# Three moves in a single-core transformer kernel: forget weights scaled later, gate logits after the third chunk, a bank sum ahead of the first convolution

## The reference, cut to what matters

```python
# first block, gated linear attention: the input projection and the gate
proj = x @ w_in
q, k, v, g, a1 = jnp.split(proj, [...], axis=-1)
log_a = jax.nn.log_sigmoid((a1 @ w_a2 + b_a).astype(jnp.float32)) / GATE_TAU
...
b = jnp.cumsum(to_chunks(log_a), axis=3)
q_dec = qc * jnp.exp(b); k_dec = kc * jnp.exp(-b); k_end = kc * jnp.exp(b_last - b)

# second block, each of 2 layers: norm, projection with the forget columns in it
u = rms_norm(h, attn_norm_w[i])
proj = u @ w_in[i]                      # f_logit: 8 of its columns

# second block, each of 2 layers: the feed-forward network
up = u @ w_up
a, g = up[..., :D_FF_2], up[..., D_FF_2:]
a = causal_depthwise_conv(a, conv_w, conv_b)
return (jax.nn.gelu(a, approximate=False) * g) @ w_down
```

## Time and profile before

| | us |
|---|---|
| median of 3 runs | 1370.71 (1370.24 to 1370.98) |
| the profiled run | 1370.33 |
| its span (first to last instruction) | 1368.6 |
| outside the span | 1.7 |

### The profile page before, as it was taken

How to read it: one execution, slowest core, us unless ns; L and a number is a source line. 1 busy time by engine, 2 the same in 40 slices (tenths; PEclk the granted TensorE clock), 3 DMA queues, 4 the chain that set the end, 5 groups by cost and what they waited for, 6 DMA issues and landing times.

```text
span 1368.6 us, 21813 instructions
## 1 busy us (share of the span) xinstructions
PE 1321.9 (97%) x8766; PEld 1187.6 (87%) x8766; DVE 915.9 (67%) x1091; ACT 667.0 (49%) x764; POOL 31.2 (2%) x52
## 2 busy tenths in 40 slices
PE   7899999998999999998999999999999999999997
PEld 6898888887986888887998989999989988999997
DVE  3746755566455765667666687777696768877775
ACT  6345544445455544445445554444655455544454
POOL 0000000000011000000200000000020000000000
PEclk9999999999999999999999999999999999999999
DMA  9534655554533455553533355555545324555520
GB/s 374 203 124 154 228 196 195 191 195 138 183 121 109 181 203 185 184 184 118 198 131 117 126 182 184 184 184 184 175 143 187 137 84 164 198 184 184 184 93 32
DMA packets 33490, 229.85 MB, mean 168 GB/s; under 512 B 3728, under 2 KB 3984, under 8 KB 6032
## 3 DMA queue, kind: packets, MB, share of 16 engines
q1 hardware_dynamic: 31536, 220.21, 45.9%
q10 hardware_dynamic: 1888, 8.68, 1.7%
HBM read 227.83 MB, written 1.05 MB: 167 GB/s over the span
## 4 chain that ended last, share of the span: by engine, by line
PE 85%; DVE 7%; ACT 3%; DMA 2%; issue 2%; SPq 0%; POOL 0%; DVEq 0%; ACTq 0%
PE ring L336 19%; PE ring L334 10%; PE ring L277 9%; PE ring L278 8%; PE ring L279 8%; PE acc L379 4%; PE acc L381 4%; PE acc L380 4%; PE acc L277 3%; PE acc L279 3%; PE acc L278 3%; DVE wlo L269 2%; DMA wf_sb<-wf 2%; PE ring L379 1%; PE ring L381 1%
## 5 line engine op out<-in xcount | busy, mean ns | idle before, releaser
L269 DVE TENSOR_TENSOR wlo<-raw,whi 128x2048 fp32r<-128x2048 f32 x207 | 474.9, 2298 | 182.5 <-ACT whi L261 182.3
L261 ACT CAST whi<-raw 128x2048 fp32r<-128x2048 f32 x207 | 393.9, 1907 | 109.3 <-PE ring L279 48.5
L336 PE MATMUL ring<-xs,whi 128*128 128x512 f32 x1184 | 423.1, 400 | 0.0
L334 PE MATMUL ring<-xs,wlo 128*128 128x256 f32 x1184 | 334.9, 283 | 6.1 <-DVE y L1502 5.9
L336 PEld LDWEIGHTS ring<-xs,whi 128*128 128x128 f32 x1184 | 224.0, 189 | 54.0
L277 PE MATMUL ring<-xs,whi 128*128 128x256 f32 x832 | 242.3, 291 | 12.6 <-DVE wlo L1539 6.4
L278 PE MATMUL ring<-xs,whi 128*128 128x256 f32 x832 | 236.9, 285 | 0.0
L279 PE MATMUL ring<-xs,wlo 128*128 128x256 f32 x832 | 236.8, 285 | 0.0
L334 PEld LDWEIGHTS ring<-xs,wlo 128*128 128x128 f32 x1184 | 225.2, 190 | 8.6 <-issue 6.5
L277 PEld LDWEIGHTS ring<-xs,whi 128*128 128x128 f32 x832 | 161.1, 194 | 17.6 <-issue 7.4
L278 PEld LDWEIGHTS ring<-xs,whi 128*128 128x128 f32 x832 | 161.1, 194 | 1.1 <-issue 1.0
(11 more groups left out here) (267 smaller groups left out, 1728.4 us busy)
## 6 DMA issues: line engine op xcount, KB each, us to landing
raw<-wstream SPq DMA_DIRECT2D x207, 1024.0 KB, 4.9
sq<-lnp ACTq DMA_DIRECT2D x4, 1024.0 KB, 4.9
cst<-consts ACTq DMA_DIRECT2D x1, 1029.0 KB, 15.1
hT<-xT SPq DMA_DIRECT2D x4, 256.0 KB, 5.0
raw<-wstream SPq DMA_DIRECT2D x4, 256.0 KB, 5.2
hT<-xtok ACTq DMA_DIRECT2D x1, 1024.0 KB, 18.8
misc<-decay ACTq DMA_DIRECT2D x1, 1024.0 KB, 4.9
out<-y SPq DMA_DIRECT2D x4, 256.0 KB, 2.3
```

The lines of the kernel that those rows point to most:

```text
L261: act.copy(whi[:, c % SPLIT, :], raw[:, c % RAW, :]).then_inc(hi_made, 1)
L269: dve.tensor_tensor(wlo[:, c % SPLIT, :], raw[:, c % RAW, :], whi[:, c % SPLIT, :].bitcast(f32), ALU.subtract).then_inc(lo_made, 1)
L334: pe.matmul(bank(b + t)[:, 0:256], wl[:, w], xhi[:, k, :], start=k == 0, stop=False, skip_group_check=True)
L336: mm = pe.matmul(bank(b + t), wh[:, w], xs[:, k, :, :].rearrange("p a s -> p (a s)"), start=False, stop=k == NT - 1, skip_group_check=True)
```

## The change

Three moves; no instruction is added or taken away.

1. On DVE the wait for the forget weights and their scaling stand behind the decayed keys (`g_dec`) and ahead of the split of chunk 9, instead of ahead of the log gates. The split of chunk 4 stands ahead of the wait for `g_ln`.
2. On PE the gate logits come after the product of chunk 2 instead of chunk 1; on ACT `gate_ln` comes after the copy of product 2, so the split of chunk 4 and that copy stand ahead of it.
3. In `ffn(L)` before the loop: on DVE the split of chunk c0+3 and the sum of the two g halves of block 0 stand ahead of `conv(0)`, and on ACT the copy of the g half stands ahead of the GELU.

```diff
             wide_product(C_GLA_IN, 12, FREE["gla_in"], 0, range(4, 8),
-                         {0: gate_input, 1: gate_logits, 7: turned_keys, 8: first_updates, 9: last_update,
+                         {0: gate_input, 2: gate_logits, 7: turned_keys, 8: first_updates, 9: last_update,
...
                 split_hi(act, c0 + 1 + AHEAD)
+                g_crossed(c0 + 1, 0)
                 gelu(0)
-                g_crossed(c0 + 1, 0)
                 high(0)
...
-            evacuate(C_GLA_IN, 12, gla_dest, {0: a1_copy, 1: gate_ln, 4: gate_exp, 7: keys_copied, 10: first_squares})
+            evacuate(C_GLA_IN, 12, gla_dest, {0: a1_copy, 2: gate_ln, 4: gate_exp, 7: keys_copied, 10: first_squares})
...
+                def g_total(i, m=0):
+                    dve.wait_ge(g_cross, m * 2 + (b + i + 1))
+                    dve.tensor_tensor(two(yf[:, 1536:2048]), main_half(2), two(yf[:, 512:1024]), ALU.add).then_inc(g_sum, 1)
+
                 def gated(c, i, m=0):
...
-                    dve.wait_ge(g_cross, m * 2 + (b + i + 1))
-                    dve.tensor_tensor(two(yf[:, 1536:2048]), main_half(2), two(yf[:, 512:1024]), ALU.add).then_inc(g_sum, 1)
+                    if i:
+                        g_total(i, m)
...
                 a_part(c0, 0)
+                split_lo(dve, c0 + 1 + AHEAD)
+                g_total(0)
                 conv(0)
                 zero_acc(rs_made, 3 * L + 2)
-                split_lo(dve, c0 + 1 + AHEAD)
                 gated(c0 + 1, 0)
...
-            for c in range(1, AHEAD + 2):
+            for c in range(1, AHEAD + 3):
                 split_lo(dve, c)
...
-            dve.wait_ge(wf_in, 16)
-            for L in range(DEPTH):
-                w = pv[:, PV["attn_w"] + 8 * L:PV["attn_w"] + 8 * L + 8].unsqueeze(2).to_broadcast([128, NT, 32])
-                ins = dve.tensor_tensor(wf_sb[:, L, :, :], wf_sb[:, L, :, :], w, ALU.mult)
-            ins.then_inc(wf_made, 1)
...
-            split_lo(dve, 2 + AHEAD)
...
             dve.tensor_tensor(kf[:, 0:1024], kf[:, 0:1024], sqf[:, 1024:2048], ALU.mult).then_inc(g_dec, 1)
+            dve.wait_ge(wf_in, 16)
+            for L in range(DEPTH):
+                w = pv[:, PV["attn_w"] + 8 * L:PV["attn_w"] + 8 * L + 8].unsqueeze(2).to_broadcast([128, NT, 32])
+                ins = dve.tensor_tensor(wf_sb[:, L, :, :], wf_sb[:, L, :, :], w, ALU.mult)
+            ins.then_inc(wf_made, 1)
             split_lo(dve, 7 + AHEAD)
```

## The result

| | us |
|---|---|
| median before | 1370.85 (1370.24 to 1371.03, 4 runs) |
| median after | 1362.46 (1362.0 to 1362.74, 4 runs) |
| ratio | 0.9939 (0.9927 to 0.9952) |
| profiled run, its span | 1362.74, 1361.0 |

A forecast was written before the change was run, and what follows sets the result against it. PE, busy 97% of the span, was taken as the bound, so only its pauses or lower-clock stretches could be won. 1370.33 - 8.15 (start) + 0.7 (networks) = 1362.9, given as 1363.0 us, range 1360.0 to 1366.0.

The forecast's parts named there:

- The start: Program start: the long pause before chunk 4 goes, chunk 5 starts at 43.6 instead of 51.75, a gain of 8.15 us.
- rival 4: Start: the forget weights are not what holds DVE, so the pause shrinks only 0.76 to 2.7 us; chance 0.04.
- The new pause: Start, before chunk 5: PE waits 1.5 us for its split; clock stays up, cost zero, bound 0 to 1.7 us.
- rival 1: Start: the clock falls over the new pause before chunk 5, price 1.7 us, giving 1364.7; chance 0.08.
- The scaling of the forget weights: DVE, ahead of chunk 9's split: hidden by the wait for its cast, costs nil, or 0.76 us without that cover.
- The networks' pause: Feed-forward networks: the pause moves from c0+3 to the down product, 3.25 us, waiting for the split of c0+4.
- rival 2: Networks: both pauses simply vanish, because the split of c0+4 is not what ends last; 1353 us; chance 0.05.
- The term of +0.7 for the networks: Two feed-forward networks: about 0.35 us lost in each, +0.7 together, bounds -0.8 to +1.0.
- I take the fall: Networks: the clock falls behind the down product's pause, full price 1.65 us; product takes 7.4 instead of 5.74 us.
- Rival 3: Networks: the down product runs longer at the lower clock, 0.8 us more each, 1364.5, up to 1366; chance 0.08.
- Rival 5: Layer norms and between layers: the shift brings clock falls at short pauses, 1.7 us each, 1371.4 and more; chance 0.03.

The follow-up runs named there:

- e4: Kernel before with only two loads swapped: the forget weights' load issued ahead of the tokens' on ScalarE's queue; 1363.23 us.
- e5: Changed kernel with the wait for the forget weights and their scaling put back ahead of the log gates; 1368.25 us.
- e1: Kernel before with moves 1 and 2, without move 3; 1364.14 us.
- e6: Changed kernel with the networks' accumulator set to zero by ScalarE instead of VectorE; 1359.18 us.
- e10: Kernel before with moves 1 and 2, without move 3, run again on one chip beside the changed kernel; 1362.33 us.
- e2: Kernel before with move 3 alone; 1370.0 us, ratio 0.9995.
- e9: The changed kernel itself, run again for more runs on one chip beside moves 1 and 2 alone; 1362.69 us.
- e11: Changed kernel with VectorE's split of chunk 5 ahead of the gate's running sums; 1360.62 us.
- e8: Changed kernel with both edits: accumulator set to zero by ScalarE, and split of chunk c0+4 ahead of the convolution; 1356.25 us.
- e3: Kernel before with move 1 alone, gate logits and gate_ln staying behind chunk 1; 1363.15 us.
- e7: Changed kernel with the split of chunk c0+4 ahead of the convolution and GELU on both engines, loops turned accordingly; 1360.47 us.
- e12: Changed kernel with three edits: ScalarE zeroing, split of c0+4 ahead of the convolution, split of chunk 5 ahead of the running sums; 1354.11 us.

## Why the prediction was right

- **The start** (forecast -8.15). Chunk 4 was expected at 36.2 without a pause and starts at 36.5; chunk 5 at 43.6 behind 1.5 us, and starts at 43.75 behind 1.32; turned keys at 60.9, and they come at 61.10. The gain there is 7.9. The missing 0.23 arose before the change has any effect: chunk 1 started 0.28 later, at 17.41 instead of 17.13. That the forget weights' load held DVE, and not one of the other three in the same wait, e4 and e5 show from both sides (rival 4 is out).
- **The new pause leaves the clock alone.** As taken: 1.00 in and behind it, here and in the six other traces that have it (e1, e6 to e10; 1.31 or 1.32 us each; rival 1 is out).
- **The scaling of the forget weights is hidden.** It ran at 56.69, and the split of chunk 9 behind it still waited 0.53 us for ACT's cast.
- **The networks' pause moves to the down product**, 3.2 us for a split, in every kernel that has move 3 and leaves DVE's chain as it is (e2, e5, e9, e11; 3.25 forecast); rival 2 is out. e6 to e8 show why: it is the length of the chain on DVE. With the zeroing taken out the pause is 1.83, with the split ahead of the convolution 2.06, with both 0.7.
- **The term of +0.7 for the networks was mis-sized.** The changed kernel's trace shows +0.28 for the two together, inside the bounds of -0.8 to +1.0. The fall came behind both pauses there, as taken, and the down product took 7.37 us against the 7.4 forecast. What doesn't hold is the reason, "I take the fall, since all four pauses of 2.0 us and more ... were followed by it": in e2 the clock did not fall behind either of the two pauses of 3.2 us. Move 3 alone measures as nothing: 0.9995 (0.9986 to 1.0005). One slip of the working is harmless: "48 such matmuls took 8.7 us" stands on a row that counts 51 in 8.75 us, so 32 take 5.5 and the price of a fall by it is 1.7 instead of 1.65.
- **Falls are not the same from run to run.** What the Trainium skill's "TensorE: Matmul & The Clock Gate" (section "What's actually happening") says of slow matmuls, that their number differs from run to run of one kernel, the traces agree with: e1 and e10 are one kernel, and in one of them the clock fell at 17.4, which cost 1.5 us by the turned keys. Rival 3, a lower clock that lasts longer, did not come in the changed kernel's trace, but it is real: in e11 the down product of the second network took 8.5 us behind its pause, at a mean clock of 0.65, and in e10 the product c0+3 of the first network took 8.5 us where it takes about 5.6 at full clock. Rival 5 did not come either: the only falls in the changed kernel's trace are those behind the pause of 2.0 us near 632 and the two of 3.2 us, and one at 1358, behind PE's last product, which the kernel before has as well (at 1366).
- **Move 2** was costed together with move 1 and I did not say what it gives alone. e3 shows that it is nothing: its 1.2 to 1.4 us of parameter wait are paid back in the pause before chunk 5.
- The sum for the profiled run, 1362.9, met 1362.74. That it is so close is partly luck: its two mis-sized terms, 0.23 too much gain at the start and 0.42 too much loss in the networks, half cancel, and one run of a kernel can lie 1 to 3 us beside another.

What stays open: whether move 3 is worth anything at all. Differences under 1 us are below what the scatter of the runs lets one see with five to ten of them. Why the clock falls behind one pause and not behind another of the same length is open too.

## What to carry to other kernels

Before a wait is moved away, write down what ends last once it is gone, engine by engine: the same sum that found 8 us at the start found that the pauses of the networks would only move on to the next operand. A small load that an engine waits for belongs ahead of a large one on the same queue; here that one swapped line gave as much as the rewritten start. Where a pause moves to the next operand, shorten the chain (give a part of it to an engine that idles) and then reorder: on top of move 3, which made nothing measurable, the shorter chain alone made 3.3 us (e6), a second reordering alone 2.0 us (e7), and both 6.2 us (e8).

## What the runs showed of the hardware

Between 1.8 and 3.2 us, how long PE stood still does not settle whether its clock goes from 2.4 to 1.2 GHz behind it. Pauses of PE of 1 us and more over the fourteen traces (before, after, e1 to e12; without the first wait of the program), and how many were followed by a fall:

| pause, us | falls |
|---|---|
| 1.06 to 1.63 | 0 of 18 |
| 1.80 to 2.65, before chunk 1 and in the networks | 4 of 11 |
| 2.01, at one place of the program (from between 629 and 640 on) | 13 of 14 |
| 2.94 to 2.96 | 10 of 10 |
| 3.20 to 3.22 | 8 of 10 |
| 3.54 to 5.68 | 3 of 3 |

A fall cost 1.6 us in the down product of the changed kernel (7.37 us against 5.74 at full clock), 2.3 us at the start of the kernel before, and 2.7 to 2.9 us in the two products of e11 and e10 that took 8.5 us. That makes the falls a large part of the scatter of these kernels: the four runs of e11 lie up to 3.5 us apart, two of mean granted clock 0.996 at 1359.5 and 1359.6 us, one of 0.994 at 1361.7, one of 0.993 at 1362.9. The 13 runs of the kernel before that stood beside e1 to e4 lie within 2.2 us. The other surprise: to write zeros into 128x2048 of the accumulator took ScalarE 1.89 us and VectorE 1.76 us plus a gap of 0.42 ahead of it that no semaphore explains. ScalarE had the time to spare: in e6 it still waits 1.87 us for VectorE before the GELU that follows.
